# Samples' top-k rounds, mask and its spreading: from the projections to slots 1 to 6 of the merge

## The chip, the cores and the metric

The kernel runs on one core of a Trainium2 chip. The metric is the device time of one launch in microseconds (us); lower is better. The engines work side by side and meet only at semaphores: TensorE (PE in the profile, its weight loads PEld), VectorE (DVE), ScalarE (ACT), GpSimd (POOL), and SyncE (SP), which here only issues DMAs.

## The reference, cut to what matters

One layer of a decoder for 512 prompt tokens and 8 sample tokens, each of which has 512 cached positions in 4 pages. For the samples the sparse attention keeps 128 of 513 positions, by the indexer's scores:

```python
dots = jnp.einsum('bqhd,bkd->bqhk', q_idx, k_idx).astype(jnp.float32) * (DH_IDX ** -0.5)
score = jnp.einsum('bqhk,bqh->bqk', jax.nn.relu(dots), w_idx.astype(jnp.float32))
score = jnp.where(causal[None], score, -jnp.inf)
_, idx = lax.top_k(score, k_sel)          # k_sel = min(256, 513 // 4) = 128
...
s = jnp.einsum('bqhd,bqkhd->bhqk', q, k_g).astype(jnp.float32) * (DH_DSA ** -0.5)
p = jax.nn.softmax(jnp.where(valid[:, None], s, -jnp.inf), axis=-1)
return jnp.einsum('bhqk,bqkhd->bqhd', p.astype(v.dtype), v_g)
```

Around it stand the combined projection, a differential attention ("d") beside the sparse one ("s"), gates, the output projection, and a two-level mixture of 32 experts. All is float32.

## The kernel before, in words

Four blocks run one after the other, each with a barrier of the engines between: `project`, `attend_prompt`, `merge`, `experts`. Each engine has one written-out order of instructions within a block.

**Projections.** 40 units (`UNITS`): eight column groups (qi, kw, ks, qs, vs, kd, qd, vd) by five token tiles, the fifth (index 4, `NT`) holding the 8 samples. TensorE makes unit u in one of three banks `z`, and can begin u only when VectorE has read unit u - 3 (`z_free`, for normed groups at L584). VectorE's `sums` (L549) and `finish` (L584 to L605) of a normed unit wait twice for GpSimd (L518, L524). From unit 15 on, each prompt unit also carries two steps of the prompt tiles' indexer scores (`extras`): TensorE L392 into two banks, ScalarE's relu, VectorE's accumulation L657, which frees the bank (`x_free`).

A top-k of 128 is 16 rounds of `take8`: MAX8 (L537) finds the 8 largest of each row, MATCH_REPLACE8 (L538) puts the value TAKEN in their places. `rounds` is a list, first in, first out: 16 rounds of the samples' scores `score_s` (8 x 513) enter at unit 13, those of prompt tile 1 (128 x 256) at unit 18, tile 2 (128 x 384) at unit 23, tile 3 (128 x 512) at unit 28. A normed prompt unit takes up to three (behind `sums`, in `finish` behind L592, and at its end), a value unit up to five at its end, a sample unit none. At the last unit `masks` turns TAKEN into 0 and all else into MASKED (L618, and L619 for the samples).

**Attention of the prompt** doesn't read the samples' scores. It makes the gate rows, and the logits of the samples against their cached keys (`sT`).

**Merge.** 16 slots (`SLOTS_A`). In slot sl TensorE makes product m = sl of the output projection (L1207) in a ring of three banks, and VectorE multiplies it by its gate (`merge_tile`, L1497, `y_read`); product m needs `y_read` of m - 3. Slots 3 to 6 also hold the values of the diff pages, slots 8 to 11 those of the DSA pages, two samples of 4 pages each (L1248). SyncE has 8 places for pages and issues page m when page m - 8 is used (`v_used`). At 32 used pages GpSimd issues both halves of `w_out` (L1176). Before slot 0 TensorE spreads the samples' mask over 64 rows with two products (L1318, L1319) and VectorE copies it to `selb` (L1649, L1650, `sel_read`). The transposed logits of branch "d" come up at the end of slot 1, of "s" at the end of slot 6 (`SOFTMAX_AT`, L1347); in the slot after it VectorE finds the largest (L1518 to L1524, for "s" adding `selb`), ScalarE takes the exponentials (L1454), VectorE the weights (L1529 to L1538), and TensorE turns them (L1353) behind the slot's product. ScalarE issues the second pair of gate loads only behind the softmax of "s".

```python
            sp.wait_ge(y_read, len(PRODUCTS))
            for e in range(2):
                for n in range(3):
                    load_expert(sp, io, s, e, n)
```

**Experts.** 32 experts with 6 MB of weights each, streamed through rings of places of 2 MB; the first loads are issued by the merge's SyncE queue, as quoted.

## Time and profile before

| | |
|---|---|
| median of 3 runs | 1198.38 us (1197.56 to 1198.66) |
| the profiled execution | 1198.17 us, span 1196.3 us |
| TensorE busy | 1038.1 us (87%) |
| VectorE busy | 439.9 us (37%) |
| ScalarE, GpSimd busy | 239.2 us (20%), 299.0 us (25%) |
| read from HBM, written | 290.09 MB, 29.72 MB |
| chain that ended last | DMA 20%, PE 16%, SP's queue 4% |

Times in the trace count from the span's start. The projections end near 288 us, the prompt's attention near 481, the merge near 685; then come the experts. Shares are averages over stages with different limits, so a stage has to be read in its own window.

### The profile page before, as it was taken

How to read it: one execution, taken by the hardware profiler on the slowest of the kernel's cores; microseconds unless marked ns; L12 is line 12 of the kernel's file. 1: busy time of each engine (PE TensorE's matmuls, PEld its weight loads, DVE VectorE, ACT ScalarE, POOL GpSimd, SP SyncE). 2: the span in 40 equal slices, each digit the busy share in tenths (PEclk: the TensorE clock that was granted, in tenths of full speed). 3: DMA queues.
4: the chain of work that ended last, by engine and by line, in shares of the span. 5: the costliest groups of instructions: out<-in, count | busy, mean ns of one | idle time of the engine just before them, and what ended most of it. 6: DMA issues, size and time to landing. Idle time of an engine off the chain costs nothing. (4 is left out here: it accounts for less than half of the span.)

```text
span 1196.3 us, 16124 instructions
## 1 busy us (share of the span) xinstructions
PE 1038.1 (87%) x5989; PEld 577.7 (48%) x5989; DVE 439.9 (37%) x1213; ACT 239.2 (20%) x542; POOL 299.0 (25%) x262
## 2 busy tenths in 40 slices
PE   6998999988999999898999579999777778777785
PEld 3644443445776777332455344555443445444342
DVE  3635788776565664421324311111110111011220
ACT  2112211211344445301024201111011110111101
POOL 1033303441554434001000012332222212222111
PEclk9998999998999999998999779999999998999998
DMA  6332022207476444788492789999999999999991
GB/s 198 92 108 81 1 98 98 89 1 252 136 237 193 122 139 159 263 318 304 125 429 85 276 320 407 393 396 390 404 402 396 402 397 407 400 405 400 409 390 54
DMA packets 82465, 304.27 MB, mean 254 GB/s; under 512 B 23138, under 2 KB 27362, under 8 KB 70226
## 3 DMA queue, kind: packets, MB, share of 16 engines
q1 hardware_dynamic: 64658, 273.47, 60.0%
q0 software_dynamic: 9824, 16.98, 5.0%
q10 hardware_dynamic: 7904, 12.78, 3.0%
q8 instruction: 48, 0.79, 0.3%
q14 instruction: 31, 0.25, 0.1%
HBM read 290.09 MB, written 29.72 MB: 267 GB/s over the span
## 5 line engine op out<-in xcount | busy, mean ns | idle before, releaser
L383 PE MATMUL p_z<-k_w,k_xT 128*128 128x512 f32 (+2 forms) x528 | 212.1, 556 | 4.9 <-DVE p_t L584 4.8
L383 PEld LDWEIGHTS p_z<-k_w,k_xT 128*128 128x128 f32 (+1 forms) x528 | 93.0, 191 | 109.5 <-issue 106.8
L841 PE MATMUL a_G<-k_xT,k_w 128*128 128x260 f32 x512 | 129.3, 397 | 0.0
L1994 DVE TENSOR_TENSOR e_hid<-e_hid,e_G 128x256 f32<-128x256 f32 x32 | 13.5, 421 | 263.1 <-ACT e_hid L1907 263.1
L841 PEld LDWEIGHTS a_G<-k_xT,k_w 128*128 128x128 f32 x512 | 94.3, 194 | 27.7 <-issue 14.5
L1912 ACT ACTIVATE e_y<-e_Y,x_share 64x512 f32<-64x512 f32 x64 | 43.7, 683 | 319.4 <-PE e_Y L1797 283.2
L936 POOL TENSOR_TENSOR k_x<-k_x 128x512 f32<-128x512 f32 x64 | 80.6, 1273 | 95.8 <-DVE k_side L999 75.8
L2035 POOL DMA_INDIRECT out_y_p<-e_y,x_table x32 | 45.1, 1408 | 205.3 <-ACT e_y L1912 143.2
L152 POOL DMA_INDIRECT k_rows<-token_rows,x_table x32 | 31.4, 981 | 179.9 <-PE e_TX L1777 165.3
L1999 DVE TENSOR_TENSOR e_hid<-e_hid,e_U 128x256 f32<-128x256 f32 x32 | 13.5, 421 | 133.4 <-PE e_U L1783 133.4
L1207 PE MATMUL g_ring<-k_oT,k_w 128*128 128x512 f32 x128 | 59.9, 614 | 0.0
L911 ACT ACTIVATE a_prob<-a_masked,a_nb 128x128 f32<-128x128 f32 (+3 forms) x64 | 36.0, 563 | 77.8 <-DVE a_nb L1013 77.8
L2038 POOL DMA_INDIRECT out_y_s<-e_y,x_to_s x32 | 45.1, 1411 | 9.7 <-issue 9.7
L1797 PE MATMUL e_Y<-k_xT,e_aT 128*64 128x512 f32 x176 | 40.2, 598 | 8.2 <-DVE e_aT L2003 8.2
L1797 PE MATMUL e_Y<-x_page,e_aT 128*64 128x512 f32 x176 | 40.2, 598 | 7.6 <-DVE e_aT L2003 7.6
L999 DVE TENSOR_REDUCE k_side<-k_x 128x8 f32<-128x512 f32 x64 | 43.1, 674 | 1.4 <-POOL k_x L936 1.4
L1783 PE MATMUL e_G<-k_w,e_xT 128*64 128x256 f32 x256 | 34.6, 426 | 10.2 <-DMA k_w<-in_w_gate 9.4
L516 POOL TENSOR_SCALAR p_rs<-p_ms 128x8 f32<-128x8 f32 (+1 forms) x20 | 3.9, 196 | 157.3 <-DVE p_ms L549 157.3
L1797 PE MATMUL e_Y<-x_w_out,e_aT 128*64 128x512 f32 x160 | 36.5, 598 | 5.4 <-DVE e_aT L2003 5.4
L1783 PE MATMUL e_U<-k_side,e_xT 128*64 128x256 f32 x256 | 33.8, 420 | 8.5 <-DMA k_side<-in_w_up 8.5
L1783 PE MATMUL e_U<-k_w,e_xT 128*64 128x256 f32 x256 | 33.6, 417 | 8.2 <-DMA k_w<-in_w_up 8.2
L524 POOL TENSOR_TENSOR p_tb<-p_t,q_rg 128x512 f32<-128x512 f32 (+1 forms) x20 | 35.4, 1771 | 18.0 <-DVE p_t L584 18.0
(354 smaller groups left out, 1494.4 us busy)
## 6 DMA issues: line engine op xcount, KB each, us to landing
k_w<-in_w_in SPq DMA_DIRECT2D x11, 2048.0 KB, 8.3
k_xT<-in_w_down SPq DMA_DIRECT2D x11, 2048.0 KB, 45.0
x_page<-in_w_down SPq DMA_DIRECT2D x10, 2048.0 KB, 44.1
x_w_out<-in_w_down SPq DMA_DIRECT2D x10, 2048.0 KB, 44.7
k_w<-in_w_gate SPq DMA_DIRECT2D x8, 2048.0 KB, 41.8
k_w<-in_w_up SPq DMA_DIRECT2D x8, 2048.0 KB
k_oT<-in_w_gate SPq DMA_DIRECT2D x8, 2048.0 KB, 44.3
k_side<-in_w_up SPq DMA_DIRECT2D x8, 2048.0 KB, 45.1
```

The lines of the kernel that those rows point to most:

```text
L383: last = nc.tensor.matmul(z[u % 3][0:p, 0:WIDTH[k]], s.xT[:, j, 128 * i:128 * i + p], s.w[:, c % 2, j, 0:WIDTH[k]], start=j == 0, stop=j = ...
L524: nc.gpsimd.tensor_tensor(tb[0:p, :].rearrange("p (h d) -> p h d", h=H), t0[0:p, :].rearrange("p (h d) -> p h d", h=H), bcast(s.rg[0:p, g, ...
L841: last = nc.tensor.matmul(G[u % 2][:, 0:HT], s.w[:, q % 2, j, 128 * c:128 * c + 128], s.xT[:, j, HT * h:HT * h + HT], start=j == 0, stop=j ...
L911: nc.scalar.activation(prob[:, n % 4, 0:w], masked[:, n % 3, 0:w], ACT.Exp, bias=nb[:, n:n + 1], scale=DH ** -0.5, accum_out=sums[:, n:n + ...
L936: nc.gpsimd.tensor_tensor(prods[:, m % 2, :], page[:, m % KEY_PLACES, :], qB[:, nq % 2, :], ALU.mult).then_inc(k_used, 1)
L999: nc.vector.tensor_reduce(s.sT[k][:, n, H * b:H * b + H], prods[:, m % 2, :].rearrange("p (h d) -> p h d", h=H), AX.X, ALU.add).then_inc(k ...
L1207: last = nc.tensor.matmul(bank[:], s.wo[k][:, j, first:first + 128], x[:, j, 0:SEQ], start=j == 0, stop=j == NB - 1)
L1783: last = nc.tensor.matmul(pair(bank[CAP * h:CAP * h + CAP, 0:HW]), xT[:, j, b, :], own(weight_row(s, n, r, b), h), start=b == 0, stop=b == ...
L1797: last = nc.tensor.matmul(bank[CAP * h:CAP * h + CAP, :], aT[:, b % 2, CAP * (b // 2):CAP * (b // 2) + CAP], weight_row(s, 2, r, b)[:, W * ...
L1912: last = nc.scalar.activation(y[j][:, W * h:W * h + W], Y[j][CAP * h:CAP * h + CAP, :], ACT.Copy, scale=s.share[CAP * h:CAP * h + CAP, e:e ...
L2035: nc.gpsimd.indirect_dma_start(out=io["y_p"], out_offset=bass.IndirectOffsetOnAxis(ap=rows, axis=0), in_=y[n][:], in_offset=None, bounds_c ...
L2038: nc.gpsimd.indirect_dma_start(out=io["y_s"], out_offset=bass.IndirectOffsetOnAxis(ap=to_s, axis=0), in_=y[n][:], in_offset=None, bounds_c ...
```

## The change

The samples' rounds and their mask leave `project`. In `merge` VectorE takes them in slots 1 to 5 (`ROUNDS_AT`: 2, 1, 5, 5 and 3 rounds, each behind the slot's merge tile and what else the slot has), then masks (`sel_masked`). TensorE waits for that at the head of slot 6, ahead of product 6, spreads the mask there into banks P and S0, and the transposes of the DSA logits at the end of slot 6 wait until VectorE has copied it (`masks_up`, at the head of VectorE's slot 6). The wait for `sel_read` in slot 0 is gone. Scores, rounds and mask are computed as before, in the same order.

```diff
--- before.py
+++ after.py
@@ -616,7 +616,6 @@
                     take8(rounds.pop(0))
                 for t in range(1, NT):
                     nc.vector.tensor_scalar(score[t - 1][:], score[t - 1][:], TAKEN, MASKED, ALU.not_equal, ALU.mult)
-                nc.vector.tensor_scalar(score_s[:], score_s[:], TAKEN, MASKED, ALU.not_equal, ALU.mult)
 
             for i in range(2):
                 scale_rows(i)
@@ -677,7 +676,6 @@
                     dve.wait_ge(x_ready, PAIRS + 3)
                     link(nc.vector.tensor_copy(score_s[:, PAST:PAST + 1], xs[PAIRS % 2][0:NS, 0:1]))
                     dve.sem_inc(x_free, 1)
-                    rounds += [score_s[:]] * TK_ROUNDS
                 for _ in range(0 if i == NT else 1 if k in NORMED else 5):
                     if rounds:
                         take8(rounds.pop(0))
@@ -1040,10 +1038,12 @@
 PLACES = 8
 
 VALUES_AT = {}
+ROUNDS_AT = {1: 2, 2: 1, 3: 5, 4: 5, 5: 3}
 for _b in range(NS // 2):
     VALUES_AT[3 + _b] = ("vd", [2 * _b, 2 * _b + 1])
     VALUES_AT[8 + _b] = ("vs", [2 * _b, 2 * _b + 1])
 SOFTMAX_AT = {1: "d", 6: "s"}
+SOFTMAX_S = 6
 OD_AT = 7
 
 PAGES = [(c, b, n) for _sl in range(SLOTS_A) for c, bs in (VALUES_AT.get(_sl, ("", [])),) for b in bs for n in range(NPAGE)]
@@ -1098,6 +1098,7 @@
         sc, pr, selb = (scp[0:R, 516 * n:516 * n + PAST + 1] for n in range(3))
         aN = dict(d=sb("aNd", [NS, R // 2]), s=sb("aNs", [NS, R]))
         dg = sb("dg", [R, R])
+        m8 = sb("m8", [NS, 8])
         mx, nb, sm, cf = (sb(n, [R, 2]) for n in ("mx", "nb", "sm", "cf"))
         od, oq, orr, orx = (sb(n, [128, NB * NS]) for n in ("od", "oq", "orr", "orx"))
         mh = sb("mh", [128, NB * NS])
@@ -1124,10 +1125,10 @@
 
         (made, g_exp, gs_exp, y_read, chain, merged_ready, raw_ready, turned, summed, x_done, x_in, sel_up, sel_read, nk_ready, nk_up,
          nk_read, sc_ready, max_ready, p_ready, weights, p_turned, a_ready, v_used, o_ready, ov_ready, ext_ready,
-         oq_ready, o_sum, orr_ready, o_rs, oT_ready, ms_ready, zeros_ready) = map(sem, (
+         oq_ready, o_sum, orr_ready, o_rs, oT_ready, ms_ready, zeros_ready, sel_masked) = map(sem, (
              "made g_exp gs_exp y_read chain merged_ready raw_ready turned summed x_done x_in sel_up sel_read nk_ready nk_up "
              "nk_read sc_ready max_ready p_ready weights p_turned a_ready v_used o_ready ov_ready ext_ready "
-             "oq_ready o_sum orr_ready o_rs oT_ready ms_ready zeros_ready").split())
+             "oq_ready o_sum orr_ready o_rs oT_ready ms_ready zeros_ready sel_masked").split())
         (wr_in, wr_ready, x_sq, pool_chain, rms, hn_ready, h_turned, hT_out, logits, differ, decided, weighed, ranked, tab_in, shares_in, tabled,
          table_ready) = map(sem, ("wr_in wr_ready x_sq pool_chain rms hn_ready h_turned hT_out logits differ decided weighed ranked tab_in "
                                   "shares_in tabled table_ready").split())
@@ -1315,10 +1316,12 @@
                     last = nc.tensor.matmul(TBw, at(k), Wk[0:p, 1, k, :], start=False, stop=k == 1, skip_group_check=True)
                 last.then_inc(tabled, 1)
 
-            nc.tensor.matmul(P[0:R, :], s.c[0:NS, C_E:C_ET], s.sel_s[:, 0:PAST], start=True, stop=True)
-            nc.tensor.matmul(O[0:R, 0:1], s.c[0:NS, C_E:C_ET], s.sel_s[:, PAST:PAST + 1], start=True, stop=True).then_inc(sel_up, 1)
             m = 0
             for sl in range(SLOTS_A):
+                if sl == SOFTMAX_S:
+                    pe.wait_ge(sel_masked, 1)
+                    nc.tensor.matmul(P[0:R, :], s.c[0:NS, C_E:C_ET], s.sel_s[:, 0:PAST], start=True, stop=True)
+                    nc.tensor.matmul(S0[0:R, 0:1], s.c[0:NS, C_E:C_ET], s.sel_s[:, PAST:PAST + 1], start=True, stop=True).then_inc(sel_up, 1)
                 v, vb = VALUES_AT.get(sl, ("", []))
                 product(m)
                 if vb:
@@ -1327,7 +1330,6 @@
                     values(v, vb[0])
                 m += 1
                 if sl == 0:
-                    pe.wait_ge(sel_read, 1)
                     pe.wait_ge(nk_ready, 1)
                     nc.tensor.matmul(O[0:R, 16:32], s.c[0:NS, C_E:C_ET], nk[:].rearrange("b c h -> b (c h)"), start=True, stop=True).then_inc(nk_up, 1)
                 if vb:
@@ -1343,6 +1345,8 @@
                     nc.tensor.matmul(S0[:, 64:64 + NB * NS], s.c[:, C_ONE:C_CM], oq[:], start=True, stop=True).then_inc(o_sum, 1)
                 if sl in SOFTMAX_AT:
                     k = SOFTMAX_AT[sl]
+                    if k == "s":
+                        pe.wait_ge(sel_read, 1)
                     for n in range(NPAGE):
                         last = nc.tensor.transpose(P[0:R, 128 * n:128 * n + 128], sT[k][:, n, :], s.ident[:])
                     last.then_inc(sc_ready, 1)
@@ -1645,10 +1649,18 @@
                 last.then_inc(shares_in, 1)
                 link(v.tensor_tensor(s.Cpre[0:p], s.Cpre[0:p], C[0:p], ALU.add))
 
-            dve.wait_ge(sel_up, 1)
-            link(v.tensor_copy(selb[:, 0:PAST], P[0:R, :]))
-            link(v.tensor_copy(selb[:, PAST:PAST + 1], O[0:R, 0:1]))
-            dve.sem_inc(sel_read, 1)
+            def take_samples(n):
+
+                for _ in range(n):
+                    link(v.max(m8[:], s.sel_s[:]))
+                    link(v.match_replace(s.sel_s[:], m8[:], s.sel_s[:], TAKEN))
+
+            def masks_up():
+
+                dve.wait_ge(sel_up, 1)
+                link(v.tensor_copy(selb[:, 0:PAST], P[0:R, :]))
+                link(v.tensor_copy(selb[:, PAST:PAST + 1], S0[0:R, 0:1]))
+                dve.sem_inc(sel_read, 1)
 
             for i, k in enumerate("ds"):
                 link(v.tensor_tensor(prod[0:NS, :], s.row["q" + k], s.row["k" + k], ALU.mult))
@@ -1660,6 +1672,8 @@
             link(v.memset(s.Cpre[:], 0.0))
             jb = lambda ap: ap.rearrange("p (j b) -> p j b", j=NB)
             for sl in range(SLOTS_A):
+                if sl == SOFTMAX_S:
+                    masks_up()
                 if sl - 1 in SOFTMAX_AT:
                     largest(SOFTMAX_AT[sl - 1])
                 if sl == OD_AT:
@@ -1692,6 +1706,9 @@
                     dve.sem_inc(nk_read, 1)
                 if sl - 1 in SOFTMAX_AT:
                     weights_turned(SOFTMAX_AT[sl - 1])
+                take_samples(ROUNDS_AT.get(sl, 0))
+                if sl == max(ROUNDS_AT):
+                    v.tensor_scalar(s.sel_s[:], s.sel_s[:], TAKEN, MASKED, ALU.not_equal, ALU.mult).then_inc(sel_masked, 1)
             samples_raw()
             add_x(0, 0)
             samples_merged()
```

## Rows read from the trace of the kernel before

**Rows 1.** The profile page: DMA share in tenths, 40 equal slices of the span

```profile
DMA  6332022207476444788492789999999999999991
```

**Rows 2.** Chain that ended last, 1100 to 1196: start, us, what

```profile
1129.53 44.20 DMA e_up<-in_w_up
```

**Rows 3.** Windows: busy time of each engine, granted clock, DMA share, GB/s

```profile
700.00:1170.00 470.00, 389.52 (x2780) 212.68 (x2778) 66.46 (x150) 54.30 (x93) 112.99 (x89) 0.97 1.00 396
```

**Rows 4.** Timeline of SyncE's queue, 590 to 600: start, us, line, what

```profile
595.27 0.34 SPq L1067 DMA_DIRECT2D k_w<-in_w_gate  x1
```

**Rows 5.** Timeline of VectorE, projections: start, us, line, what [idle before <-releaser]

```profile
98.35 0.42 DVE L604 TENSOR_TENSOR p_y<-p_ta,p_tb 128x256 f32<-128x256 f32 x1 [1.23 <-POOL p_tb L524]
...
115.81 0.48 DVE L657 SCALAR_TENSOR_TENSOR t_sel<-p_relu,p_wi,k_c 128x256 f32<-128x256 f32 x1 [0.23 <-DVE p_y L605]
...
157.10 0.68 DVE L537 MAX8 p_m<-k_sel_s 8x8 f32<-8x513 f32 x1
...
158.59 0.68 DVE L537 MAX8 p_m<-k_sel_s 8x8 f32<-8x513 f32 x1
...
184.45 0.56 DVE L537 MAX8 p_m<-t_sel 128x8 f32<-128x384 f32 x1
...
185.70 0.42 DVE L567 COPY k_rows<-p_zs 8x512 f32<-8x512 f32 x1
...
286.36 0.41 DVE L619 TENSOR_SCALAR k_sel_s<-k_sel_s 8x513 f32<-8x513 f32 x1
286.70 0.41 DVE L567 COPY k_rows<-p_zs 8x512 f32<-8x512 f32 x1
```

**Rows 6.** Timeline of TensorE, projections and the next block's first product

```profile
116.41 1.85 PE L392 MATMUL p_xs<-p_kiT,p_qiT 64*128 64x256 f32 x4 [5.28 <-DVEq L661]
...
146.66 0.92 PE L392 MATMUL p_xs<-p_kiT,p_qiT 64*128 64x384 f32 x4
...
156.30 1.67 PE L392 MATMUL p_xs<-p_kiT,p_qiT 64*128 64x384 f32 x4 [1.23 <-DVEq L661]
...
165.40 1.39 PE L392 MATMUL p_xs<-p_kiT,p_qiT 64*128 64x384 f32 x4
...
193.76 2.55 PE L392 MATMUL p_xs<-p_kiT,p_qiT 64*128 64x512 f32 x4 [2.00 <-DVEq L661]
...
251.49 7.11 PE L383 MATMUL p_z<-k_w,k_xT 128*128 128x512 f32 x16 [3.37 <-DVE p_t L584]
...
288.69 0.80 PE L854 MATMUL a_S<-t_Tkd,t_Tqd 64*128 64x128 f32 x4 [4.35 <-PEq L168]
```

**Rows 7.** Windows behind three gaps of TensorE; the clock is third from the end

```profile
250.00:251.00 1.00, 0.00 (x0) 0.00 (x0) 0.35 (x1) 0.00 (x0) 0.52 (x1) 1.00 0.00 0
113.00:115.00 2.00, 0.00 (x0) 0.00 (x0) 1.90 (x5) 0.00 (x0) 1.29 (x1) 0.55 1.04 403
195.00:197.00 2.00, 2.00 (x3) 0.50 (x2) 1.93 (x5) 1.11 (x2) 0.20 (x2) 0.53 0.00 0
```

**Rows 8.** Timeline of TensorE, merge

```profile
491.53 3.60 PE L1207 MATMUL g_ring<-k_oT,k_w 128*128 128x512 f32 x8
496.85 0.46 PE L1353 MATMUL g_P<-k_c,g_scp 64*128 64x64 f32 x4 [1.73 <-DVE g_dg L1538]
...
517.96 3.70 PE L1207 MATMUL g_ring<-k_oT,k_w 128*128 128x512 f32 x8
...
528.96 0.63 PE L1347 MATMUL g_P<-k_c,k_side 128*64 128x128 f32 x4
...
546.28 1.56 PE L1248 MATMUL x_O<-x_page,k_side 128*32 128x512 f32 x2 [2.76 <-DMA x_page<-in_cache_dsa_v]
```

**Rows 9.** Timeline of VectorE, merge

```profile
492.47 0.68 DVE L1518 COPY g_scp<-g_P 64x512 f32<-64x512 f32 x1
...
501.25 0.69 DVE L1497 TENSOR_TENSOR x_merged<-g_ring,k_xT 128x512 f32<-128x512 f32 x1 [2.51 <-PE g_ring L1207]
```

**Rows 10.** Timeline of GpSimd, 528 to 529

```profile
528.38 0.96 POOL L1176 DMA_DIRECT2D x_w_out<-in_w_out  x1 [44.76 <-PE x_O L1248]
```

## The prediction

> **What bounds the kernel now.** I read the slices of the page first, to see which stage waits for what. From the 25th of 40 slices on the DMA line stands at 9 nearly to the end [rows 1]: the experts' stage is a stream of weights. The chain that ended last says the same: its longest pieces are weight loads, the last one 44.20 us [rows 2], and the windows give 396 GB/s with a DMA share of 1.00 over 470 us [rows 3]. That stream cannot be shortened by this change, but its start can be moved: SyncE issues the first expert load only when VectorE has read all the merge's products, at 595.27 us, and later ones as the merge's sums finish [rows 4]. So whatever the stages ahead of 595 us win or lose should arrive at the end one for one. The edit acts at two places ahead of it, the projections (to 288 us) and the merge (from 481 us), so I read the timelines of VectorE and TensorE there, always asking for whom TensorE waits.
>
> **What leaves the projections.** 16 rounds on the samples' scores, 513 wide. One is MAX8, a value load and MATCH_REPLACE8; two begin 1.49 us apart [rows 5], though only 8 partitions are used. That is 16 x 1.49 = 23.8 us of VectorE. TensorE is the busier engine here, so only its waits for VectorE count:
> - Near 111 us TensorE stands 5.28 us, until VectorE's accumulation at 115.81 frees a score bank [rows 5, 6]. In the chain to that row stand three rounds. The one before sample unit 14 counts whole (1.49). The one behind the head sums hides in the wait for GpSimd's powers, and the one behind the cosine product all but hides in the wait for GpSimd's sine product, which is 1.23 us where no round fills it [rows 5]: 1.49 - 1.23 = 0.26. Gain 1.75.
> - At 156.30 TensorE waits 1.23 and its four score products take 1.67 where 0.92 is their time, and at 165.40 1.39 [rows 6]. Twelve sample rounds on units 15 to 18 made VectorE late. Without them it is about 4 us earlier there (1.75 from above, 1.49 for the round at unit 17's end, 0.26 in unit 18's finish, and unit 18's last round is now one of tile 1, 0.5 shorter), and both waits go: 1.23 + 0.75 + 0.47 = 2.45.
> - Then the queue of rounds refills: the prompt tiles' rounds start once their scores exist, so units 21 to 28 hold as many as before, and the later waits for VectorE stay (251.49 [rows 6]). Four rounds are 512 wide instead of 384 (1.49, by the 513 row, against 1.25 [rows 5]), three of them not hidden: 3 x 0.24 = 0.7 given back.
> - At the end VectorE's copy of the last unit ends at 287.1 [rows 5], 2.8 us behind TensorE's last product (288.69 - 4.35 = 284.34 [rows 6]), because it still had a backlog and, between tiles' masks and copy, the samples' mask (0.3 from start to start). The mask goes, and the rounds end a unit earlier. What must follow that product is ScalarE's four small copies (1.15 in the trace) and the 0.41 copy: about 1.1 won.
> Attention starts 1.75 + 2.45 - 0.7 + 1.1 = 4.6 us earlier. The ends: 3.5 if a wait just moves to the next unit, 6.5 if a low-clock stretch (below) is spared too. Attention itself (rounds, mask and score row of the samples aren't read there) shifts as a whole.
>
> **What comes to the merge's start.** The two selection products (some 1.2 us of TensorE) and VectorE's two copies behind them move to slot 6. That buys nearly nothing: the first merge tile waits for ScalarE's gate rows, still on their way from 481 to 489 us. Only the second tile, which waited for its product at 491.4, comes 0.75 earlier. Two rounds are put behind it, ahead of the diff softmax: 2.99 - 0.75 = 2.25 us later than 492.47 [rows 9]. From that row to the turned weights at 496.85 [rows 8] everything is one chain (VectorE, ScalarE's exp, VectorE), and TensorE already waits 1.73 for it, so all 2.25 count. TensorE's gap becomes some 4.8 us, from 494.3 to 499.1.
>
> **The clock.** A gap costs more than itself. After the 5.28 us gap the granted clock stood at 0.50 to 0.55, its 1.2 GHz level, and it fell to 0.53 even behind the 2.00 us gap ahead of 193.76; yet in the 3.37 us gap before 251.49 it stayed at 1.00 [rows 6, 7]. I take a fall behind each of the new gaps of about 5 us: TensorE then works some 3.5 us at half speed, losing 1.75 (bounds 0 and 2.6, from the 3.4 to 6.9 us that such stretches last in this trace). The Trainium skill (TensorE: Matmul & The Clock Gate, HAM oscillation) has the array cold only behind long gaps. By it the 2.00 us gap would have been harmless, the row says it was not; for the new gaps of 5 us both give the same fall, and if neither came the sum would be 3.5 us less, which is a rival below.
>
> **The rounds of slots 3 to 5.** This is the term that decides. VectorE's merge of tile 3 starts at 501.25 [rows 9]; now at 501.25 + 2.25 + 1.75 = 505.25. From there VectorE has to do 3 merge tiles (0.73 each), 13 rounds (19.4) and the mask (0.45) before the new semaphore: 22.0 us, so 527.3. TensorE would come to slot 6 at 517.96 + 4.0 = 522.0 [rows 8]. It waits about 5.3 us, at the head of slot 6, and behind this wait in its queue stand product 6, the last 8 diff pages' values, the transposes of the DSA logits, and through them the page places that SyncE refills. VectorE's merge tiles 4 and 5 come 1 to 3 us late too, but TensorE needs them three products later: nothing.
> What the wait gives back: slot 6 took 11.0 us from 517.96 to the transposes at 528.96 [rows 8], much of it for pages on their way. All 8 pages of this slot land while TensorE waits. What is left is the selection (0.7 warm), the product 3.65, values 1.9 (as in slots 3 and 5), the new rows 1.0: 7.25, and 1.75 of low clock = 9.0. The copies of the spread mask (0.83) lie beside product 6. Transposes at 527.3 + 9.0 = 536.3, against 528.96: **7.4 us later**. Bounds: 3.9 with no low clock, 9.1 with the long one.
> Behind this, GpSimd issues w_out when the 32nd page is used (528.38 [rows 10]), ScalarE the second pair of gate loads only after the DSA softmax. Both move along, so the stretch where TensorE waits for pages at a full DMA (546.28 [rows 8]) moves too. Before, the first pages of slot 8 were under way before w_out; now all 8 are issued beside it. Up to 1.05 MB more at 396 GB/s [rows 3] is 2.7 us; I take 1.0 (0 to 2.7), as half of the load that it competes with isn't needed until 592 us. The Trainium skill (DMA: Bandwidth & Descriptors, Queues, rings and completion order) lets each DMA engine go round robin between queues: 2.1 MB of pages beside w_out would need 10.6 us by an estimate from that (4.2 MB at 396 GB/s), against 10 from the 32nd page to slot 8's values, so the same 1 us; no row here shows it.
>
> **The sum.** -4.6 + 7.4 + 1.0 = +3.8 us. The profiled execution took 1198.17 us (span 1196.3 and 1.9 around it), 0.2 under the median of the runs: 1198.17 + 3.8 = 1202.0.
>
> **Rivals.**
> - *Gaps without the clock* (0.2). The rows at 3.37 us show that a gap can pass at full clock. Both merge gaps then cost only themselves: -4.6 + 3.9 + 0 to 1.0 = about 0, 1197.5 to 1199. Against it: every gap over 4 us in the trace was followed by a low clock.
> - *The merge hides the rounds, faster* (0.14). VectorE was idle 8.85 and 4.8 us between the merge tiles of slots 3 to 6, and the stretch near 546 us is bound by DMA; if page loads, gates and w_out reach their end by bandwidth alone, a late slot 6 is paid out of that wait, and the projections' 4.6 stays: 1194 to 1196. It decides once the merge loses under 2.2 us. For it: the wait at 546.28 is for pages [rows 8]. Against: these loads are released by slot 6 itself; and VectorE's free time from 501.25 to 517.96 is 16.7 - 2.2 = 14.5 us, for 19.9 us of new work.
> - *The queue behind slot 6 grows* (0.08): long low clock twice, 2.7 us of DMA backlog: 1205 to 1208.
> - *The projections give nothing* (0.05): VectorE's wait just moves to later units. Then +8.4 stands alone: 1206 to 1207.
> My forecast has 0.53. Its own range is 1200.3 to 1204.
>
> **How the numbers follow.** About 0.2% (2.4 us) is what measurement of this kernel can tell. Slower by over 2.4: most of the forecast (0.47) and the two upper rivals (0.13) = 0.60. Same: the rest of the forecast, the first rival and a little of the second = 0.27. Faster: 0.13. The range 1197.5 to 1206.5 leaves out the faster case and the top.
>
> **What would show it.** Right: attention's first product 4 to 5 us earlier than 288.69; the wait near 111 us shortened by under 2, that at 156 gone; in the merge a TensorE wait of about 5 us for VectorE ahead of the turned diff weights, and one of about 5 us for the mask (tensor_scalar on the samples' scores) ahead of the selection products, no page waits in slot 6, w_out issued some 3 us later than 528.4; first expert load about 4 us later than 595.27. Wrong: VectorE done with the mask before TensorE is at slot 6; a clock that stays at 1.00 over both gaps; page waits after slot 8 much shorter; or the start of the experts' stream moved while the end isn't.

## The result, and the profile after

The changed kernel takes 1210.77 us (median of 4 runs, 1209.52 to 1212.52) against 1198.52 us of the kernel before on the same chip (1197.56 to 1200.75): a ratio of 1.0096, 95% interval 1.0078 to 1.0115. It is slower by about 12 us, or 1%. The prediction had +3.8 us and a range of 1197.5 to 1206.5. The profiled execution took 1210.56 us with a span of 1208.7 us, 12.4 more than before; its times are compared below.

The end again follows the start of the experts' stream. SyncE issues the first expert load 13.45 us later than in [rows 4], for a span that is 12.4 us longer. In all twelve kernels below the span moved with this load too, within 2.6 us:

```profile
608.72 0.34 SPq L1067 DMA_DIRECT2D k_w<-in_w_gate  x1
```

**Projections**, on TensorE (start, us, line, what, and in brackets the idle time before it with its releaser). The first group answers to the row at 116.41 of [rows 6], and so on down:

```profile
115.57 1.85 PE L392 MATMUL p_xs<-p_kiT,p_qiT 64*128 64x256 f32 x4 [3.54 <-DVEq L660]
...
189.70 2.97 PE L392 MATMUL p_xs<-p_kiT,p_qiT 64*128 64x512 f32 x4 [1.95 <-DVEq L660]
...
192.60 9.26 PE L383 MATMUL p_z<-k_w,k_xT 128*128 128x512 f32 x16
...
249.33 9.88 PE L383 MATMUL p_z<-k_w,k_xT 128*128 128x512 f32 x16 [4.16 <-DVE p_t L584]
...
286.25 0.80 PE L852 MATMUL a_S<-t_Tkd,t_Tqd 64*128 64x128 f32 x4 [3.25 <-PEq L168]
```

The wait near 111 us is 1.74 us shorter, those near 156 and 165 are gone, the last one is 1.1 shorter. But the wait near 250 grew from 3.37 to 4.16 us, and the same 16 products behind it took 9.88 us where they took 7.11. Of these 3.6 us about 2 came back by the last product, mostly because two waits are gone that stood behind these products before:

```profile
259.74 7.13 PE L383 MATMUL p_z<-k_w,k_xT 128*128 128x512 f32 x16 [0.71 <-DVE p_t L584]
...
268.04 7.13 PE L383 MATMUL p_z<-k_w,k_xT 128*128 128x512 f32 x16 [0.73 <-DVE p_t L584]
```

Attention's first product comes 2.44 us earlier, not 4.6. But this execution was 0.9 us late before the change could act: a product that stands ahead of the first round (L409) starts at 80.33 us here and at 79.42 before. Counted from it the projections are 3.35 us shorter.

**Merge**, on TensorE, against [rows 8]. The line numbers moved by a few: L1208 are the products, L1249 the values, L1357 the turned weights, L1323 the spreading products, L1351 the transposes of the logits:

```profile
486.82 3.60 PE L1208 MATMUL g_ring<-k_oT,k_w 128*128 128x512 f32 x8
499.79 0.69 PE L1357 MATMUL g_P<-k_c,g_scp 64*128 64x64 f32 x4 [9.37 <-DVE g_dg L1542]
500.40 0.38 PE L1359 MATMUL g_P<-g_dg,k_c 64*8 64x64 f32 x2
500.71 5.37 PE L1208 MATMUL g_ring<-k_oT,k_w 128*128 128x512 f32 x8
...
520.50 2.35 PE L1249 MATMUL x_O<-x_page,k_side 128*32 128x512 f32 x16
527.94 1.94 PE L1323 MATMUL g_P<-k_sel_s,k_c 8*64 8x512 f32 x2 [5.09 <-DVE k_sel_s L1711]
529.67 0.31 PE L1324 MATMUL g_S<-k_sel_s,k_c 8*64 8x1 f32 x2
529.92 6.12 PE L1208 MATMUL g_ring<-k_oT,k_w 128*128 128x512 f32 x8
535.97 1.92 PE L1249 MATMUL x_O<-x_page,k_side 128*32 128x512 f32 x16
537.82 1.04 PE L1252 MATMUL x_O<-k_rows,g_aNd 8*32 8x512 f32 x2
538.80 0.62 PE L1351 MATMUL g_P<-k_c,k_side 128*64 128x128 f32 x4
```

Both new waits are where they were looked for. The one for the mask has the forecast size (5.09 against 5.3), the one ahead of the turned weights twice its own (9.37 against 4.8). Behind each, eight products that take 3.70 us elsewhere took 5.37 and 6.12. The windows over these two stretches (length, busy time of TensorE, weight loads, VectorE, ScalarE, GpSimd, then granted clock, DMA share, GB/s) show the clock at its lower level (0.50) for most of the time, and a DMA that moves almost nothing:

```profile
497.00:508.00 11.00, 8.21 (x31) 3.23 (x32) 6.40 (x25) 6.58 (x14) 0.00 (x0) 0.68 0.01 3
530.00:538.00 8.00, 8.00 (x25) 2.83 (x26) 1.52 (x3) 0.00 (x0) 0.00 (x0) 0.70 0.02 7
```

Two windows of before, over the products of slots 3 and 6, for comparison:

```profile
498.00:502.00 4.00, 4.00 (x20) 1.45 (x22) 1.44 (x9) 2.65 (x7) 0.00 (x0) 1.00 0.27 98
518.00:522.00 4.00, 4.00 (x14) 1.54 (x12) 0.23 (x1) 0.00 (x0) 0.00 (x0) 1.00 0.74 219
```

All 8 places hold pages that nobody has used, so nobody asks for more. The bytes come later, when TensorE needs them: two windows behind slot 6 have the DMA full and TensorE idle for some 40% of the time, and in the second of them its clock is at the lower level.

```profile
549.00:554.00 5.00, 2.85 (x4) 0.21 (x3) 0.00 (x0) 0.00 (x0) 0.00 (x0) 0.79 1.04 388
554.00:559.00 5.00, 3.13 (x4) 0.36 (x4) 0.00 (x0) 0.00 (x0) 0.00 (x0) 0.50 1.04 390
```

Slot 8's 16 value products, which took 1.92 us in a row before, now stretch over nearly 12, because their pages come one by one:

```profile
547.80 2.13 PE L1249 MATMUL x_O<-x_page,k_side 128*32 128x512 f32 x10
551.87 1.91 PE L1249 MATMUL x_O<-x_page,k_side 128*32 128x512 f32 x2 [1.93 <-DMA x_page<-in_cache_dsa_v]
554.82 1.92 PE L1249 MATMUL x_O<-x_page,k_side 128*32 128x512 f32 x2 [1.04 <-DMA x_page<-in_cache_dsa_v]
557.78 1.91 PE L1249 MATMUL x_O<-x_page,k_side 128*32 128x512 f32 x2 [1.05 <-DMA x_page<-in_cache_dsa_v]
```

Before, the pages were short one slot further on ([rows 8], the row at 546.28), so most of this is the same wait in another place.

**VectorE** in the merge, from the first tile to the end of the rounds, against [rows 9]:

```profile
490.72 1.29 DVE L1501 TENSOR_TENSOR x_merged<-g_ring,k_xT 128x512 f32<-128x512 f32 x2 [7.88 <-issue]
...
492.42 0.68 DVE L1655 MAX8 g_m<-k_sel_s 8x8 f32<-8x513 f32 x1
...
495.41 0.68 DVE L1522 COPY g_scp<-g_P 64x512 f32<-64x512 f32 x1
...
506.22 0.69 DVE L1501 TENSOR_TENSOR x_merged<-g_ring,k_xT 128x512 f32<-128x512 f32 x1 [3.02 <-PE g_ring L1208]
...
527.47 0.42 DVE L1711 TENSOR_SCALAR k_sel_s<-k_sel_s 8x513 f32<-8x513 f32 x1
```

From merge tile 3 to the end of the mask it is 527.89 - 506.22 = 21.7 us (22.0 forecast). The first tile comes late because ScalarE's gate rows land late. They were issued at 478.99, and their first use is at 489.89, 10.90 us on; before it was 8.07 us on (481.00, 489.07):

```profile
478.99 0.97 ACTq L1400 DMA_DIRECT2D k_xT<-gate_rows  x2
...
489.89 0.21 ACT L1407 ACTIVATE g_gate_s<-k_xT 128x8 f32<-128x8 f32 x1 [8.61 <-DMA k_xT<-gate_rows]
```

**The account**, in us later (+) or earlier (-) than before, from these rows. "Transposes" are those of the DSA logits at the end of slot 6. "Squares' sum" is TensorE's product behind the values of slot 9 (L1343 before, L1345 after), at 557.46 us before and at 570.24 after:

| stretch | forecast | measured |
|---|---|---|
| up to the issue of the gate rows | -4.6 | -2.0 |
| gate rows' landing | 0 | +2.8 |
| two rounds ahead of the diff softmax | +2.25 | +2.1 |
| low clock in slot 3 | +1.75 | +2.0 |
| VectorE's rounds to the mask, beyond TensorE's own time (21.7 - 16.7) | +5.3 | +5.0 |
| slot 6 from the mask to the transposes (11.0 before) | -2.0 | -0.1 |
| transposes to the squares' sum in slot 9 | +1.0 | +2.95 |
| on to the first expert load | 0 | +0.7 |
| the experts' stage | 0 | -1.05 |
| span | +3.8 | +12.4 |

The forecast's terms are rounded and add up to 3.7 here. The -2.0 of the first line holds the 0.9 us by which this execution was late before the change could act.

### The profile page after: what moved, and what is told of

It reads as the page before. It is cut to its first block and busy times, and to the rows that moved or that the text cites. A ratio compares the mean times of both kernels' runs of the same rounds, so it can differ in the third digit from the quotient of the medians.

```text
span 1208.7 us, 16123 instructions
## 1 busy us (share of the span) xinstructions
PE 1042.5 (86%) x5989; PEld 579.0 (48%) x5989; DVE 439.8 (36%) x1213; ACT 238.7 (20%) x542; POOL 298.7 (25%) x262
## 5 line engine op out<-in xcount | busy, mean ns | idle before, releaser
L383 PE MATMUL p_z<-k_w,k_xT 128*128 128x512 f32 (+2 forms) x528 | 216.2, 564 | 4.2 <-DVE p_t L584 4.2
L1208 PE MATMUL g_ring<-k_oT,k_w 128*128 128x512 f32 x128 | 63.7, 646 | 1.1 <-PEq L718 1.1
L1208 PEld LDWEIGHTS g_ring<-k_oT,k_w 128*128 128x128 f32 x128 | 25.3, 207 | 33.0 <-issue 32.8
```

Of the source, the lines that this page charges most:

```text
L383: last = nc.tensor.matmul(z[u % 3][0:p, 0:WIDTH[k]], s.xT[:, j, 128 * i:128 * i + p], s.w[:, c % 2, j, 0:WIDTH[k]], start=j == 0, stop=j = ...
L1208: last = nc.tensor.matmul(bank[:], s.wo[k][:, j, first:first + 128], x[:, j, 0:SEQ], start=j == 0, stop=j == NB - 1)
```

## The experiments

Twelve kernels ran. "Of the merge" means counted from the issue of the first gate rows: before, the squares' sum in slot 9 is at 76.46 us of it, in the changed kernel at 91.25. Medians carry the comparison; positions come from one profiled execution each. In experiments 3 and 5 that one is 3.6 and 4.7 us faster than the median of its kernel, in 2 and 9 it is 2.7 and 2.2 slower, so there a position and a median aren't to be added up.

**1. The projections' half alone.** Of before, without the samples' rounds and mask; the merge spreads the raw scores in the mask's place, so this kernel leaves that selection out.

```
-                    rounds += [score_s[:]] * TK_ROUNDS
-                nc.vector.tensor_scalar(score_s[:], score_s[:], TAKEN, MASKED, ALU.not_equal, ALU.mult)
```

> The kernel before without the samples' 16 rounds and their mask anywhere; the merge is as before and spreads the raw scores in place of the mask. Theory A (the trace of the changed kernel): the projections give back only 2 to 3 us of the 23.8 us of VectorE, because the wait near 250 us grows past 4 us and drops TensorE's clock; the end is 2 to 3 us ahead of before (1195.5 to 1196.5). Theory B (the step of the prediction): 4.6 us, so 1194. Rival C (nothing is won, the gain seen is chance): within 1 us of before.

1196.15 us (1192.01 to 1199.26, 10 runs) against 1198.35: ratio 0.9977 (0.996 to 0.9994), a gain of 2.2 us. Its merge is that of before (squares' sum at 76.42), and its projections have the same rows as the changed kernel:

```profile
250.37 9.93 PE L383 MATMUL p_z<-k_w,k_xT 128*128 128x512 f32 x16 [4.17 <-DVE p_t L584]
```

In the profiles of all nine kernels that leave the rounds out of the projections and change nothing else there, the wait near 250 us is 4.16 to 4.18; in the three that keep them it is 3.34 to 3.37. So theory A holds: the wait has grown past 4 us, the clock falls, and the median gains 2.2 us. The interval of that gain is wide, 0.7 to 4.8 us, so the median alone doesn't rule 4.6 out; the rows say where the rest went. By subtraction the merge's half costs about 14.5.

**2. The merge's half alone.** The changed kernel, with the rounds and mask kept in the projections too (the merge works them again on the finished mask).

```
                     dve.sem_inc(x_free, 1)
+                    rounds += [score_s[:]] * TK_ROUNDS
...
+                nc.vector.tensor_scalar(score_s[:], score_s[:], TAKEN, MASKED, ALU.not_equal, ALU.mult)
```

> The changed kernel with the 16 rounds and the mask kept in the projections as well, so that in the merge they run a second time, over a finished mask (what is computed for the samples changes). The merge's half of the change alone, against the kernel before. Theory A: the merge's half costs 14 to 15 us and the projections' half wins 2 to 3, so this ends at 1212 to 1214. Theory B (prediction): the merge costs 8.4, so 1207. Rival C: half of the cost is an accident of the order in which queues share the DMA at the merge's start; then the first gate rows land 8 us after their issue, as before, and this ends near 1209 to 1210.

1210.7 us (1209.25 to 1213.35, 4 runs), ratio 1.0104 (1.0086 to 1.0123): the whole loss is there with nothing taken from the projections. That is 12.35 us, 10 to 15 by the interval: less than theory A's 14 to 15, far more than the prediction's 8.4. Rival C doesn't hold either, since the gate rows were used only 10.79 us after their issue. Squares' sum at 91.84, the two waits 7.56 and 4.66. Against the changed kernel the median shows no price of the doubled rounds, the profiled execution 2.8 us; with four runs each, the intervals hold both. So the medians of 1 and 2 leave the projections' gain anywhere from nothing to 4.8 us.

**3. The rounds without a wait.** Of before, with 16 rounds and a mask on a scratch tile of [8, 513] in slots 1 to 5; selection and its spreading stay as they were, and nobody reads the scratch tile.

```
+ROUNDS_AT = {1: 2, 2: 1, 3: 5, 4: 5, 5: 3}
...
+                for _ in range(ROUNDS_AT.get(sl, 0)):
+                    link(v.max(m8[:], other[:]))
+                    link(v.match_replace(other[:], m8[:], other[:], TAKEN))
```

> The kernel before, mask spread ahead of slot 0 as before, with 16 more rounds and a mask on a scratch row tile put where the changed kernel has them, slots 1 to 5; TensorE waits for none of them. It leaves the stall at slot 6 out and keeps VectorE's load. Theory A: the stall at slot 6 is what costs most; left are 2.99 us in the diff softmax and the clock behind that gap, so 1202 to 1205. Rival B: VectorE's load itself, by late merge tiles and a late largest value of the DSA branch, is the cost, whoever waits: then 1209 to 1213.

1205.22 us (1201.64 to 1206.55, 4 runs), ratio 1.0066 (1.0046 to 1.0087). That is 6.9 us above the kernel before, just past theory A's 1205. Squares' sum at 81.65, 5.2 us later than before, though no engine waits for the rounds themselves. The turned diff weights, behind the two rounds of slot 1, are 3.0 us late, and the clock drops behind their wait:

```profile
500.31 0.68 PE L1356 MATMUL g_P<-k_c,g_scp 64*128 64x64 f32 x4 [4.72 <-DVE g_dg L1541]
```

The gap is 4.72 us, as forecast (4.8) for a kernel whose gate rows land on time (7.38 us here). The low clock behind the gap then makes the stretch up to the first values 2.8 us longer (7.04 for 4.23). From the turned weights at 500.31 to the transposes at 534.44 it takes 34.1 us for 32.1 before, so the 13 rounds of slots 3 to 5 add nothing that the clock doesn't explain. The two rounds ahead of the diff softmax cost about half of the loss; the other 13 cost only where somebody waits for them.

**4. TensorE kept at work over the two waits.** The changed kernel, with 9 and 5 products that nobody reads (into bank B) ahead of the two waits.

```
+                    for j in range(5):
+                        nc.tensor.matmul(B[:], s.wo[0][:, j % 4, 0:128], s.oT["d"][:, j % 4, 0:SEQ], start=True, stop=True)
                     pe.wait_ge(sel_masked, 1)
```

> The changed kernel with TensorE kept at work over its two new waits by products that nobody reads: 9 (8.3 us) ahead of the wait for the diff weights in slot 2, and 5 (4.6 us) ahead of the wait for the mask in slot 6. Theory A (each gap drops the clock and this costs 2 us at slot 2 and 2.4 at slot 6): product 3 and product 6 take 3.7 us in place of 5.4 and 6.1, and the end comes 4 to 5 us ahead of the changed kernel, 1206 to 1207. Rival B (the clock is only beside the point, the stretch behind is set by page loads): the products are quick, the end moves by less than 1.5 us.

1205.47 us (1203.14 to 1205.92, 4 runs), ratio 1.0059 (1.0039 to 1.008): 5.3 us ahead of the changed kernel, with more work in it, as theory A had it and a little more. Squares' sum at 84.72. The mask is ready 2.0 us earlier, counted from VectorE's first merge tile (34.75 against 36.75); the product behind the wait takes 3.70 again, slot 6 7.5 us instead of 10.86, and the windows read 1.00:

```profile
526.88 1.07 PE L1325 MATMUL g_P<-k_sel_s,k_c 8*64 8x512 f32 x2 [0.34 <-DVE k_sel_s L1716]
527.79 0.22 PE L1326 MATMUL g_S<-k_sel_s,k_c 8*64 8x1 f32 x2
527.94 3.70 PE L1208 MATMUL g_ring<-k_oT,k_w 128*128 128x512 f32 x8
```

```profile
496.00:506.00 10.00, 9.10 (x35) 3.60 (x37) 7.22 (x27) 6.58 (x14) 0.00 (x0) 1.00 0.26 97
526.00:534.00 8.00, 7.66 (x32) 2.44 (x30) 2.31 (x5) 0.00 (x0) 0.08 (x1) 1.00 0.49 156
```

So the clock behind the two waits is about 5.3 us of the loss, against the 3.5 in the sum. The bare delays stay: the mask is still what slot 6 waits for, now with the fillers in the gap.

**5 to 7. The rounds ahead of slot 0, the spreading behind slot 6, and both.** 5: five rounds go where VectorE waits for the gate rows. 6: the wait and the two spreading products go behind product 6 and its values, VectorE's copies to the head of slot 7.

```
-ROUNDS_AT = {1: 2, 2: 1, 3: 5, 4: 5, 5: 3}
+ROUNDS_AT = {-1: 5, 2: 1, 3: 3, 4: 5, 5: 2}
...
+            take_samples(ROUNDS_AT.get(-1, 0))
```

```
                     if k == "s":
+                        pe.wait_ge(sel_masked, 1)
+                        nc.tensor.matmul(P[0:R, :], s.c[0:NS, C_E:C_ET], s.sel_s[:, 0:PAST], start=True, stop=True)
...
                         pe.wait_ge(sel_read, 1)
```

> The changed kernel with other places for the rounds: 5 ahead of slot 0, where VectorE waits some 8 us for the first gate rows, none in slot 1, then 1, 3, 5 and 2 in slots 2 to 5. Same work, same waits. Theory A (the loss is where the rounds don't fit): slot 2's gap is 1 to 2 us again as before; in slots 3 to 5 VectorE has 17.5 us of work for 16.7 us of time, so the wait at slot 6 is under 1.5 us; both falls of the clock go; 10 to 12 us ahead of the changed kernel, 1199 to 1201. Rival B (20 us more of VectorE in the merge cost the same wherever they stand): within 3 us of the changed kernel.

> The changed kernel with the wait for the mask and the two spreading products moved from the head of slot 6 to its end, just ahead of the transposes of the DSA logits; rounds where the change has them. Theory A (what is queued behind the wait makes it dear: product 6, 8 pages' values, SyncE's places): the work of slot 6 now runs beside VectorE's rounds, the wait is under 1 us, spread and copy (about 1.7 us) stand bare; 5 to 7 us ahead of the changed kernel, 1204 to 1206. Rival B (the DSA softmax is what is late, by the rounds, and the place of the wait does not matter): within 2 us of the changed kernel.

> Rounds as in the run with 5 ahead of slot 0, and the spread at the end of slot 6. Theory A: the remaining wait at the head of slot 6 is under 1.5 us and goes, the bare spread and copy cost 1.7: within 1.5 us of that run, so 1198 to 1201. Rival B: both moves win on their own, 1194 to 1197, ahead of the kernel before.

| kernel | us (range, runs) | ratio (95%) | the two waits | squares' sum |
|---|---|---|---|---|
| 5 | 1200.09 (1194.75 to 1204.55, 10) | 1.0001 (0.998 to 1.0021) | 6.02, 2.26 | 81.70 |
| 6 | 1201.88 (1197.87 to 1203.39, 10) | 1.002 (1.0004 to 1.0037) | 8.03, none | 83.52 |
| 7 | 1199.43 (1194.65 to 1200.39, 10) | 0.9997 (0.998 to 1.0014) | 6.02, none | 80.08 |

Each move alone wins back 9 to 11 of the 12 us, both together hardly more than the better one, well inside the spread: they buy out the same loss. The order alone made the difference between 1.0096 and 1.000.

The totals of 5 and 7 came out as theory A had them, the waits didn't. In 5 slot 2's gap was to be 1 to 2 us and slot 6's wait under 1.5; they are 6.02 and 2.26, and the eight products behind the first still take 5.04 where 3.70 is their time. Counted in the merge alone all three are still behind the kernel before: its squares' sum is at 76.46, theirs are 5.2, 7.1 and 3.6 us later, and the projections' gain makes up for most of it. In 6 the gain was to be 5 to 7 and is 8.9. Its spreading finds the mask ready; what is left is the first wait with eight products at 6.06 behind it, waits of 0.58 and 1.05 us for pages, and 1.0 for VectorE's copy.

**8. w_out issued at 24 pages used, not 32.**

```
-            pool.wait_ge(v_used, NPAGE * NS)
+            pool.wait_ge(v_used, 3 * NPAGE * NS // 4)
```

> The changed kernel with GpSimd's two w_out loads (4 MB) released when 24 pages are used in place of 32, so that they fill the time in which the DMA stands idle while TensorE waits at slot 6. Theory A (loads held back by slot 6 come back as a backlog of 2 to 3 us around slots 9 and 10): from the last transposes of the DSA logits to the sum of the squares the time shrinks by at least 3 us, and the end by 3 to 5 us, 1206 to 1208. Rival B (w_out does not compete with anything that TensorE waits for): within 1.5 us of the changed kernel.

1206.52 us (1202.98 to 1210.13, 7 runs), ratio 1.0052 (1.0028 to 1.0075): about 4 us better than the changed kernel, as theory A had it, squares' sum at 88.73. From the transposes to the squares' sum it takes 22.7 us, where the changed kernel takes 31.4 and before 28.5; but the last diff pages are now late in slot 6 (two waits of 1.16 us, and a low clock), and the transposes come 6.2 us later. So w_out does compete with what TensorE waits for here, and moved ahead it pays most of its price ahead: of the 8.7 us that this stretch gains 6.2 are lost in slot 6.

**9 and 10. Why do the gate rows land late?** 9 keeps the old head of the merge as well (the two products and two copies, on raw scores, read by nobody). 10 holds GpSimd's 2 MB load of the DSA output weights until the first gate rows are in.

```
+            nc.tensor.matmul(P[0:R, :], s.c[0:NS, C_E:C_ET], s.sel_s[:, 0:PAST], start=True, stop=True)
...
+            link(v.tensor_copy(selb[:, 0:PAST], P[0:R, :]))
```

```
+            pool.wait_ge(gate_in[0], 16)
             pool.dma_start(s.wo[1],
```

> The changed kernel with the two spreading products and VectorE's two copies also at the merge's head, as before the change, on the raw scores and read by nobody (the later ones are what counts). In three traces without that head the first gate rows landed 10.1 to 10.9 us after their issue, in three with it 7.1 to 8.1. Theory A (the head's absence is what lets something get ahead of the gate rows): they land at 7 to 8.5 us, the first merge tile starts as early as before, and the end is 0 to 3 us ahead of the changed kernel. Rival B (what decides is where the program's instructions lie or in what order they are fetched, not this work): landing stays above 9.5 us and the end is 0 to 1 us behind the changed kernel.

> The changed kernel with the 2 MB load of w_o_dsa held back until the first gate rows are in, so that only the pages run beside them. Theory A (the merge's first stretch is bound by the first gate rows, and what they lose to the other queues comes out whole): they land 6 to 8 us after their issue, diff softmax and slot 3 come 2 to 4 us earlier, and the end 2 to 4 us ahead of the changed kernel. Rival B (TensorE or the queue of rounds is as late anyway, or w_o_dsa then misses slot 8): within 1 us.

9: 1210.77 us (1210.48 to 1213.01, 4 runs), ratio 1.0111 (1.0089 to 1.0134). The gate rows are used 7.68 us after their issue, as theory A had it, but the time stays, at the lowest end of its 0 to 3 us. The head costs TensorE and VectorE what the landing gives: the first product behind it takes 5.40 us, VectorE waits 1.22 for the second tile's product, and the mask is only 1.0 us earlier. 10: 1208.06 us (1201.83 to 1208.84, 4 runs), ratio 1.0076 (1.0045 to 1.0106). As theory A had it, they are used after 7.26 us; the first wait shrinks to 5.74 and the squares' sum comes at 86.59. So the late landing is real in the merge's positions. What it is worth is 2.7 us by the median of 10 and nothing by that of 9, where the head takes it back; the runs of 10 spread over 7 us.

**11 and 12. Better orders.** 11 is experiment 5 with the round at the end of each `qd` unit of the projections left for later. 12 is experiment 7 with that and the early w_out.

```
-                for _ in range(0 if i == NT else 1 if k in NORMED else 5):
+                for _ in range(0 if i == NT or k == "qd" else 1 if k in NORMED else 5):
```

> The run with 5 rounds ahead of slot 0, and in the projections no round at the end of the units of group qd: their four prompt units hold two rounds each, and the prompt tile's last rounds move to the value units behind. Theory A (the 4.2 us wait near 250 us and its fall of the clock ate half of what the projections had won): the wait is under 2 us, no fall, and the end is 2 to 4 us ahead of that run, 1195 to 1197. Rival B (the backlog then ends in the last units and the barrier is as late): within 1 us of it.

> All that won: 5 rounds ahead of slot 0, spread at the end of slot 6, two rounds in the qd units, w_out released at 24 pages. Theory A: 4 to 7 us ahead of the kernel before, 1191 to 1194. Rival B (w_out early only takes bandwidth from pages that TensorE now waits for, as its stall at slot 6 is gone): level with the run above.

11: 1194.9 us (1193.09 to 1196.96, 12 runs) against 1197.72: ratio 0.998 (0.997 to 0.9991), the fastest of all. The forecast was 2 to 4 us ahead of experiment 5; by the ratios it is 2.5. The wait near 250 us is 1.29 and the clock stays up:

```profile
244.08 7.10 PE L383 MATMUL p_z<-k_w,k_xT 128*128 128x512 f32 x16 [1.29 <-DVE p_t L584]
```

Attention starts at 278.23, 8 us before the changed kernel's, but 4.65 before experiment 5's (282.88); the rest is what the next section tells of 5 and 6. Its merge still costs more than that of before: squares' sum at 83.34, the wait for the mask 2.70, with the product behind it at 5.40:

```profile
514.20 1.07 PE L1323 MATMUL g_P<-k_sel_s,k_c 8*64 8x512 f32 x2 [2.70 <-DVE k_sel_s L1712]
515.10 0.22 PE L1324 MATMUL g_S<-k_sel_s,k_c 8*64 8x1 f32 x2
515.25 5.40 PE L1208 MATMUL g_ring<-k_oT,k_w 128*128 128x512 f32 x8
```

12: 1198.43 us (1195.5 to 1203.47, 12 runs), ratio 1.0012 (0.9998 to 1.0026). Neither text for it held: it was to come to 1191 to 1194, or level with 11, and is 3.5 us behind 11. The moves do not add up; with w_out ahead of the last diff pages, slot 6's values are late, and the spreading, now behind them, comes at 61.17 of the merge, where experiment 7 had it at 51.35.

## Why the prediction was wrong

The direction, the two places and most of the mechanism came out as forecast; the size did not: +3.8 forecast, +12 measured. Four steps failed: the low clock at slot 6, the clock behind the wait near 250 us, the gate rows taken to land as before, and the backlog behind slot 6. Point by point:

- **Right.** The wait near 111 us (3.54, a gain of 1.74 for 1.75). The waits at 156 and 165 us gone. The two rounds ahead of the diff softmax (+2.1 for +2.25). The term said to decide, VectorE's 22.0 us of rounds (21.7), and the wait of 5.3 at slot 6 (5.09). No waits for pages in slot 6. The end follows the experts' first load.
- **Projections, -4.6.** The step that failed is "the later waits for VectorE stay (251.49)". The wait near 250 grew by 0.8, and the clock, at 1.00 behind 3.37 us, fell to 0.50 behind 4.16: 2.8 us more for the same 16 products. The prediction had written that every gap over 4 us was followed by a low clock, but did not ask whether the 512-wide rounds would carry this one over 4, though its own numbers do: 3.37 and the 0.7 that it gave back make 4.07. Up to there the gain was all it should be: the score products at 179.56 come 4.0 us earlier than before. The next 1.4 us are lost behind the wait at 189.70 (2.97 for four score products and 9.26 for the next 16, where before had 2.55 and 8.25). Experiment 11 shows the wait near 250 to be the rounds' own.
- **What luck has to do with it.** The clock falls behind the wait at 189.70 in some executions and not in others, with the same wait. Nine kernels have the changed kernel's projections. In the seven where it fell, attention starts 205.5 to 206.6 us behind the L409 product (at 80.33 in the changed kernel); in the two where it stayed at 1.00 (5 and 6) 203.5 and 203.8; in the three that keep the rounds 208.7 to 209.3. So the half is worth about 3 us with that fall, and some 5.5, more than forecast, without it. Experiment 5's rows there, with 2.02 and 7.13 for the changed kernel's 2.97 and 9.26:

```profile
188.29 2.02 PE L392 MATMUL p_xs<-p_kiT,p_qiT 64*128 64x512 f32 x4 [1.95 <-DVEq L660]
190.24 7.13 PE L383 MATMUL p_z<-k_w,k_xT 128*128 128x512 f32 x16
```

- **The gate rows, 0.** "The first merge tile waits for ScalarE's gate rows, still on their way from 481 to 489 us" took their landing as fixed. It moved to 10.90 us behind the issue (+2.8). Of its value, see experiments 9 and 10; why it moved stays open.
- **The clock, 1.75 each.** Mis-sized. Slot 3 lost 2.0. Slot 6, forecast at 9.0 us, took 10.86; at full clock it takes 7.5 (experiment 4; 7.25 forecast), so the clock cost 3.4 there, beyond the bound of 2.6. The bound was a slip of its own: the prediction takes it from low stretches of 3.4 to 6.9 us, and 6.9 us of work at half speed lose 3.45, not 2.6. Its product took 6.12 for 3.70, its spreading products 2.25 for 1.29. Both falls together are 5.4 us by these rows and 5.3 by the median of experiment 4, against 3.5.
- **The backlog, +1.0.** +2.95 from the transposes to the squares' sum, just above its bound of 2.7. The mechanism was the forecast one (all 8 pages of slot 8 issued beside w_out); the step that failed is the choice of 1.0, on the ground that half of w_out isn't needed until 592 us. The DMA share is 1.04 where TensorE waits for these pages, and experiment 8 shows that w_out issued elsewhere shortens the stretch. That the 2.95 us are all bytes (1.15 MB at 389 GB/s, where the bound had 1.05) is an estimate, not shown: some of it is TensorE at 0.50 again.
- **The rivals.** Three of them are refuted: both merge gaps had their low clock, the late slot 6 was not paid out of the page waits behind it (that stretch took 2.95 us more), and the projections gave something. "The queue behind slot 6 grows" was nearest (1205 to 1208), and the end was still 3 us beyond. All the large errors lie on the same side, and it takes every one of them (projections, gate rows, clock in slot 3, slot 6, backlog): 2.6 + 2.8 + 0.25 + 1.9 + 1.95 is 9.5, with the smaller lines of the account (-0.15, -0.3, +0.7, -1.05) 8.7 of the 8.6 that are missing.

Each line of the account rests on one execution of each kernel. The start of attention differs by 5 us between the profiles of the nine kernels with the same projections (282.88 to 287.90). Their middle, 287.25, against 289.1 for the three that keep the rounds, gives 1.9 us, near experiment 1's 2.2; up to 2.8 us of the spread are there before 83 us, ahead of the first round.

## What to carry to other kernels

Before moving work into "idle" slots of an engine, look for what is behind it in order there: two rounds ahead of a softmax cost themselves and a low clock (experiment 3), and five of them put where the engine waited for a load made the first tile 0.1 us late when the load was slow (experiment 5) and 1.5 us late when it was quicker (experiment 7). Rounds in the gaps behind cost nothing as long as nobody waited for them (experiment 3). When a wait on TensorE grows, charge it three times: itself, the slow products behind it, and the loads that its consumer would have released meanwhile. And a wait that is just short of a size that was already followed by a low clock deserves its own line in the sum, however small its growth.

## What the runs showed of the hardware

- The length of a gap alone did not tell whether the clock falls. In the same place, behind gaps of 1.92 to 2.00 us, it fell to 0.50 in ten of the fourteen profiles (the four score products took 2.48 to 2.97 us), and in four it stayed at 1.00 (experiments 2, 5, 6 and 11; they took 2.02). The 3.37 us before 251.49 [rows 6] passed at 1.00, while the 3.35 us in the same place of experiment 2 were followed by 0.50 and 8.80 us for 16 products that took 7.11 before. The gaps of 4.16 us and more looked at here were followed by 0.50 each time. The Trainium skill (TensorE: Matmul & The Clock Gate, HAM oscillation) names long gaps as what the clock falls behind; the falls behind some 2 us speak against that, the longer gaps agree.
- Filler products nobody reads, over two waits, made the kernel 5.3 us faster (experiment 4).
- A load of 1 MB issued beside two other queues was first used 7.14 to 8.07 us after its issue in the four profiles with the spreading at the merge's head (before, experiments 1, 3 and 9), and 9.09 to 10.92 in nine without it. Only with GpSimd's 2 MB load held back was it 7.26 without the head. The bytes moved in the first 12 us are alike (3.98 MB before, 4.03 after). That the other queues' traffic matters is shown; why the two small products at the head do is not, and stays open.
